# First layer of a two-layer encoder trunk: attention heads placed between quarters of the input and output projection

## What is computed

```python
h = rms_norm(x, ev_attn_norm)
proj = h @ ev_w_in                                # 1024 -> 2304 columns
a_q, a_k, a_v, b_q, b_k, b_v = jnp.split(proj, IN_SPLITS, axis=-1)
# mixer A: 8 query heads on 2 key heads, 64 wide, this and the previous chunk of 64, ALiBi, a sink per head
#   sc = (norm(q) . norm(k)) / 8 - slope * |i - j|;  p = exp(sc - m) / (sum + exp(sink - m));  o = p @ v
# mixer B: 8 heads, this chunk and all earlier ones, learned relative bias; softmax; o = p @ v
x = x + jnp.concatenate([out_a, out_b], axis=-1) @ ev_w_out
h = rms_norm(x, ev_ffn_norm)
x = x + swiglu(h, ev_w_gate, ev_w_up, ev_w_down)  # 1024 -> 2816 -> 1024
```

## Time and profile before

| | value |
|---|---|
| median of three runs | 1464.49 us (1462.91 to 1468.63) |
| the profiled execution, its time | 1464.81 us |
| its span, first to last instruction | 1462.9 us |
| TensorE busy share of the span | 95% |
| mean granted TensorE clock | 0.979 of full |
| last matmul of the input projection ends near | 67.6 us |
| first matmul of the output projection | 117.75 us |
| output projection ends near | 139.87 us |

### The profile page before, as it was taken

How to read it: one execution, slowest core, us unless ns; L and a number is a source line. 1 busy time by engine, 2 the same in 40 slices (tenths; PEclk the granted TensorE clock), 3 DMA queues, 4 the chain that set the end, 5 groups by cost and what they waited for, 6 DMA issues and landing times.

```text
span 1462.9 us, 19333 instructions
## 1 busy us (share of the span) xinstructions
PE 1387.6 (95%) x6469; PEld 1136.6 (78%) x6469; DVE 1168.6 (80%) x1452; ACT 1047.8 (72%) x1359; POOL 118.3 (8%) x181
## 2 busy tenths in 40 slices
PE   7999999998598599999999999999999999999997
PEld 5757788887466488888888888888888888888885
DVE  4775555545694699899989989989998998998996
ACT  4585544446494488787887887888788788788786
POOL 0100000000350530000000000000000000000000
PEclk9999999999799699999999999999999999999998
DMA  9806554212806499999999999999999999999980
GB/s 343 296 1 230 174 201 144 72 55 73 314 2 249 163 363 386 378 382 376 372 386 371 398 357 377 404 348 395 389 371 383 375 371 386 373 388 367 376 342 14
DMA packets 133186, 429.52 MB, mean 294 GB/s; under 512 B 4194, under 2 KB 11533, under 8 KB 133149
## 3 DMA queue, kind: packets, MB, share of 16 engines
q1 hardware_dynamic: 127696, 416.82, 75.2%
q0 software_dynamic: 2624, 9.47, 2.5%
q10 hardware_dynamic: 2828, 2.75, 0.6%
HBM read 422.73 MB, written 6.29 MB: 293 GB/s over the span
## 4 chain that ended last, share of the span: by engine, by line
PE 84%; issue 6%; DVE 5%; ACT 3%; DMA 1%; POOL 1%; ACTq 0%; SPq 0%; DVEq 0%; POOLq 0%
PE bank L604 26%; PE bank L606 26%; PE bank L605 26%; PE bank L566 2%; DVE w_lo L1264 1%; PE bank L669 1%; PE bank L697 1%; ACT w_hi L878 1%; PE bank L686 1%; PE bank L530 1%; DMA xres<-in_x_dram 1%; PE bank L680 1%; ACT hT_hi L906 0%; PE bank L679 0%; ACT h L916 0%
## 5 line engine op out<-in xcount | busy, mean ns | idle before, releaser
L1194 DVE TENSOR_TENSOR w_lo<-ring,w_hi 128x1024 fp32r<-128x1024 f32 x544 | 645.8, 1220 | 39.9 <-ACT w_hi L815 22.1
L815 ACT ACTIVATE w_hi<-ring 128x1024 fp32r<-128x1024 f32 x544 | 573.3, 1063 | 134.8 <-PE bank L606 134.5
L604 PE MATMUL bank<-w_hi,hT_hi 128*128 128x512 f32 (+3 forms) x1104 | 425.6, 385 | 8.3 <-DVE w_lo L1188 2.9
L605 PE MATMUL bank<-w_hi,hT_lo 128*128 128x512 f32 (+3 forms) x1104 | 423.9, 384 | 0.0
L606 PE MATMUL bank<-w_lo,hT_hi 128*128 128x512 f32 (+3 forms) x1104 | 423.8, 384 | 0.0
L604 PEld LDWEIGHTS bank<-w_hi,hT_hi 128*128 128x128 f32 x1104 | 208.5, 189 | 50.9 <-DVE w_lo L1264 4.5
L606 PEld LDWEIGHTS bank<-w_lo,hT_hi 128*128 128x128 f32 x1104 | 208.5, 189 | 40.7
L605 PEld LDWEIGHTS bank<-w_hi,hT_lo 128*128 128x128 f32 x1104 | 208.6, 189 | 40.1
L1264 DVE TENSOR_TENSOR w_lo<-ring,w_hi 128x1024 fp32r<-128x1024 f32 (+3 forms) x124 | 144.0, 1173 | 102.0 <-ACT w_hi L878 101.8
L878 ACT ACTIVATE w_hi<-ring 128x1024 fp32r<-128x1024 f32 (+3 forms) x124 | 121.1, 987 | 115.2 <-PE bank L606 110.1
L604 PE MATMUL bank<-w_hi,aT_hi 128*128 128x512 f32 x474 | 189.2, 399 | 10.0 <-issue 5.6
(11 more groups left out here) (246 smaller groups left out, 1175.1 us busy)
## 6 DMA issues: line engine op xcount, KB each, us to landing
ring<-in_od_e_gate_dram SPq DMA_DIRECT2D x57, 2048.0 KB, 9.4
ring<-in_od_e_up_dram SPq DMA_DIRECT2D x56, 2048.0 KB, 9.6
ring<-in_od_e_down_dram SPq DMA_DIRECT2D x56, 2048.0 KB, 9.8
ring<-in_ev_w_gate_dram SPq DMA_DIRECT2D x5, 2048.0 KB, 7.9
ring<-in_ev_w_up_dram SPq DMA_DIRECT2D x5, 2048.0 KB, 9.5
ring<-in_ev_w_down_dram SPq DMA_DIRECT2D x5, 2048.0 KB, 7.9
ring<-in_ev_w_in_dram SPq DMA_DIRECT2D x3, 2048.0 KB, 21.9
ring<-in_ev_w_out_dram SPq DMA_DIRECT2D x2, 2048.0 KB, 19.4
```

The lines of the kernel that those rows point to most:

```text
L604: pe.matmul(dst, hi, whi, start=first, stop=False)
L605: pe.matmul(dst, lo, whi, start=False, stop=False)
L815: act.activation(e_hi_at[place_of(q)], eights(ring[:, i % RING, j * QUARTER:(j + 1) * QUARTER]), ACT.Copy).then_inc(hi_ready, 1)
L1194: dve.tensor_tensor(e_lo_at[place_of(q)], eights(ring[:, i % RING, j * QUARTER:(j + 1) * QUARTER]), e_hi_at[place_of(q)].bitcast(F32), ALU ...
```

## The change

1. The input projection's columns are cut 512, 512, 512, 256, 512 (`IN_COLS`), so that everything but the B values is there after quarter 15. The first 16 quarters run as before, then `heads0()` replaces `attention(0, HEADS0)` on each engine. It puts the last four quarters of the input projection behind steps 0 to 3, and the eight quarters of the output projection behind steps 7, 9, 11, 13, 15, 17 and 20 (`SLOT`).
2. The output projection goes by rows: a quarter is 128 rows (two heads) by all 1024 columns, and its sums stay in banks 4 to 7 for all eight quarters. It waits only for its own two heads.
3. Queries and keys are transposed two heads at a time: a tile is 128 columns wide. With that, 26 transposes take the place of 64. The 16 heads share one bank for scores (bank 1), one for transposed q and k, one for transposed probabilities and one for outputs, since banks 4 to 7 are taken. A new semaphore, `score_taken`, holds the scores of a head until VectorE has read those of the head before.
4. The queries of mixer A are no longer multiplied by their norm; VectorE multiplies the scores by it together with adding the distance, in two instructions, and the slope goes into ScalarE's exponential.
5. The mask is added to the bias by VectorE between quarters 8 and 11 (`add_mask`), not by GpSimd.
6. The residual sums behind the output projection and behind the feed-forward part are made by halves: VectorE adds the left half when its last matmul is done (`first_half`). The order inside a quarter is changed to suit.
7. In `norm(1)` and `norm(2)` the first quarters of the next stage are split before the squares of the norm (`SPLIT_FIRST`).
8. The feed-forward pieces start at ring place 3, not 2, because place 2 is used as scratch for squares.

The core of the diff follows: the tables and the plan; `out_quarter` and `heads0` of TensorE; the end of a step of `heads0` on ScalarE and VectorE; `add_mask` and the residual sums on VectorE; the early split in `norm` on both.

```diff
+ORDER0 = (0, 1, 4, 5, 2, 3, 6, 7, 8, 9, 10, 11, 12, 13, 14, 15)
+TILE_STEP = {0: 0, 1: 1, 4: 2, 5: 3, 8: 4, 10: 5, 12: 6, 14: 7}
+IN_COLS = ((0, NW), (NW, NW), (2 * NW, NW), (3 * NW, NW // 2), (3 * NW + NW // 2, NW))
+SLOT = {0: (16,), 1: (17,), 2: (18,), 3: (19,),
+        7: (20,), 9: (21,), 11: (22,), 13: (23,), 15: (24,), 17: (25,), 20: (26, 27)}
...
-        add("out", cols(w["w_out"], j * NW, NW), KD, NW, j)
-    place = 2
+        add("out", w["w_out"][0, j * NW:(j + 1) * NW, :].rearrange("(k p) n -> p k n", p=P), 4, D, j, "rows", j)
+    place = 3
...
+            def out_quarter(q):
+                pe.wait_ge(o_lo, max(ORDER0.index(2 * k), ORDER0.index(2 * k + 1)) + 1)
+                hi, lo = (aT_hi, aT_lo) if k < 4 else (hT_hi, hT_lo)
+                product(q, lambda t, half: bank[4 + 2 * t + half], lambda _, t: hi[:, k, t * P:(t + 1) * P],
+                        lambda _, t: lo[:, k, t * P:(t + 1) * P])
...
+            def heads0():
+                for i in range(STEPS0):
+                    if i in TILE_STEP:
+                        for t in range(TB):
+                            mm = pe.transpose(bank[0][:, t * P:(t + 1) * P], q_pair(u, t), ident)
+                        if turns_k(u):
+                            for t in range(TB):
+                                mm = pe.transpose(bank[0][:, SEQ + t * P:SEQ + (t + 1) * P], k_pair(u, t), ident)
+                    n = i - 1
+                    if 0 <= n < HEADS0:
+                        pe.wait_ge(qkT_ready, 2 * u + 2)
+                        if n:
+                            pe.wait_ge(score_taken, n)
+                        pe.matmul(bank[1][:, 0:P], q[:, 0:P], k[:, 0:P], start=True, stop=True)
+                        pe.matmul(bank[1][:, P:LANES], q[:, P:SEQ], k, start=True, stop=True).then_inc(scored, 1)
+                    n = i - 4
+                    if 0 <= n < HEADS0:
+                        pe.wait_ge(p_ready, n + 1)
+                        if n:
+                            pe.wait_ge(pT_ready, n)
...
+                    for q in SLOT.get(i, ()):
+                        if q < pieces[4]["q1"]:
+                            in_quarter(q)
+                        else:
+                            out_quarter(q)
...
+                    for q in SLOT.get(i - 1, ()):
+                        if ends_piece(q):
+                            in_evict(quarters[q][0])
+                        split_to(q + LEAD)
...
+            def add_mask(raw, c0, keys):
+                m = cst[:, c0:c0 + keys][:, ::-1].unsqueeze(1).to_broadcast([P, B_HEADS, keys])
+                dve.tensor_tensor(raw, raw, m, ALU.add).then_inc(bias_ready, 1)
...
-                dve.wait_ge(quarter_used, p["q1"])
                 for half in range(2):
+                    if half == 0:
+                        dve.wait_ge(first_half, 2)
+                    else:
+                        dve.wait_ge(quarter_used, p["q1"])
                     for t in range(TB):
                         xs = xres[:, t, half * NW:(half + 1) * NW]
                         dve.tensor_tensor(xs, xs, bank[4 + 2 * t + half][:, :], ALU.add).then_inc(x_added, 1)
...
+        SPLIT_FIRST = {1: "ffn", 2: "dq"}
+                if n in SPLIT_FIRST:
+                    split_to(pieces[stage_pieces(SPLIT_FIRST[n])[0]]["q0"] + LEAD)
```

More of the change, by code:

```diff
@@ L97, in gain_rows @@
         g[row, 0:HD] = inputs[name][0]
+        g[row, HD:2 * HD] = inputs[name][0]
     for row, name in ((G_CQ, "od_q_norm"), (G_CK, "od_k_norm")):
@@ L132, in add @@
         first = len(quarters)
-        for k in range(0, nk, per):
+        for k in ROW_ORDER.get((stage, c), range(0, nk, per)):
             quarters.append((len(pieces), k, min(per, nk - k)))
@@ L356, in o_place, with o_place0, o_psum0, ends_piece @@
             return dst[r:r + 64, m // 2, :]
+        def o_place0(first, second, g):
+            r = 64 * (g % 2)
+            return (first if g < A_HEADS else second)[r:r + 64, g // 2, :]
+        def o_psum0(n):
+            r = 64 * (ORDER0[n] % 2)
+            return bank[3][r:r + 64, 0:SEQ]
+        def ends_piece(q):
+            return quarters[q][0] < 5 and q + 1 == pieces[quarters[q][0]]["q1"]
+        def slope(g):
+            return 2.0 ** (-8.0 * (g + 1) / A_HEADS)
+        def kT_of(u):
+            return kT0[:, 0 if u < A_KV * 2 else (u + 1) % 2, :]
+        def q_pair(u, t):
+            c = 2 * u * HD if u < A_HEADS // 2 else B_Q + (2 * u - A_HEADS) * HD
+            return proj[:, t, c:c + 2 * HD]
+        def in_copy(i, t):
+            n = lin[i]["n"]
+            dst, src = dest["in"](t, i, n), bank[4 + 2 * (i % 2) + t][:, 0:n]
+            if i == 0:
+                dst = dst.rearrange("p (g two d) -> p two g d", two=2, d=HD)
+                src = src.rearrange("p (two g d) -> p two g d", two=2, d=HD)
+            return dst, src
+        def k_pair(u, t):
+            c = A_K if u == 0 else B_K + (2 * u - A_HEADS) * HD
+            return proj[:, t, c:c + 2 * HD]
+        def v_of(n, t):
+            g = ORDER0[n]
+            c = A_V + g // (A_HEADS // A_KV) * HD if g < A_HEADS else B_V + (g - A_HEADS) * HD
+            return proj[:, t, c:c + HD]
+        def turns_k(u):
+            return u == 0 or u >= A_HEADS // 2
         def gate_bank(c):
@@ L421, in trunk @@
                   "uq": (2, lat_rinv, 1), "ukv": (4, lat_rinv, 1)}
+        HEAD_SUMS0 = 5
+        SPLIT_FIRST = {1: "ffn", 2: "dq"}
+        ROW_ENDS = [pieces[stage_pieces(s)[-1]]["q1"] - 1 for s in ("out", "ffn")]
         X_ADDS = {0: 0, 1: 4, 2: 8, 3: 12}
@@ L445, in _ @@
                     sp.wait_ge(pv_done, HEADS0)
+                if p["stage"] == "ffn" and p["place"] == 2:
+                    sp.wait_ge(head_ss, HEAD_SUMS0)
                 dst = ring[:, p["place"], 0:p["nk"] * p["n"]].rearrange("p (k n) -> p k n", k=p["nk"])
@@ L626, in flags @@
             def flags(p, k):
+                if p["kind"] == "rows":
+                    return k == 0 and p["c"] == 0, k == p["nk"] - 1 and p["c"] == 1
                 if p["kind"] != "down":
@@ L739, in _ @@
             turn_norm(0)
-            projection("in", sT(hT_hi), sT(hT_lo))
-            pe.wait_ge(queries_ready, 1)
-            attention(0, HEADS0)
-            pe.wait_ge(o_lo, HEADS0)
-            projection("out", sT(hT_hi), sT(hT_lo))
+            for q in range(IN_FIRST):
+                in_quarter(q)
+            heads0()
             turn_norm(1)
```

334 lines of the change are left out of this document (261 added, 73 removed).

## The result

The changed kernel takes 1459.45 us (median of 10 runs, 1456.13 to 1461.91) against 1463.70 for the kernel before beside it (10 runs). The ratio is 0.9957, 95% interval 0.9943 to 0.9972: faster by 0.3 to 0.6%, some 6 us by the ratio, while the two medians lie 4.3 us apart. The forecast was 1454.5. The profiled execution took 1459.23 us with a span of 1457.4, where the one of before had 1464.81 and 1462.9.

What follows compares the result with a forecast made beforehand. TensorE, busy 95% of the span, was taken as the bound. -8.7 us up to the output projection's end and -1.5 behind the feed-forward part made -10.2, giving 1454.5 us; own range 1452 to 1457, full range 1450.5 to 1461.

Steps and rivals of the forecast that it cites:

- rival (a): Heads, steps 4 to 7: TensorE's clock falls again, costing 3.4 us, total 1458; chance 0.15.
- if the clock is 0.50 in that stretch: Sign that the forecast is wrong: granted clock at 0.50 between 56 and 80 us, where nothing below 1.00 was expected.
- The ledger of the input projection, heads and output projection: Those three stages: 99.2 us dense plus 2.7 and 1.1 of stalls, 103.0 against 111.74, so -8.7 us.
- all of steps 4 to 7: First heads: TensorE waits 2.7 us before quarter 20, of which 1.7 for the single scores bank.
- in the tail: Last heads: probabilities of head 13 come 0.6 us late and head 15's wait 0.5, together 1.1 us.
- A pair of steps and a quarter: Steps 8 to 20: 7.6 us of TensorE against 6.0 of VectorE, so no stall.
- The clock: Input projection to output projection: granted clock assumed 1.00 throughout, so the old low stretch's 3.4 us count within -8.7.
- The halves and the early split: Behind the feed-forward part: 1.2 us from adding by halves, 0.3 from the early split, together -1.5 us.
- The mask: Input projection: 3.7 us on VectorE, quarter 15's split just in time, no stall; relieving VectorE of GpSimd's contention gains 0.
- (c): Heads: single banks cost a handover of 0.3 us per step, 6.3 us over 21 steps, total 1461; chance 0.13.
- (d): Head loop: eleven uncovered splits cost 25 us, total 1480; chance 0.06.
- (e): Heads: output projection quarters fill nothing, only transposes (4.6 us) and 1.5 are gained, near 1458.5; chance 0.04.

Runs made afterwards that it cites:

- Experiment 11: The changed kernel run once more, unaltered: 1458.73 us (11 runs); its profiled run had the same wait but no fall of the clock.
- experiment 1: Changed kernel plus five 512-column matmuls that nothing reads, ahead of the wait in head step 6: 1456.23 us, ratio 0.9935 to the kernel before.
- experiment 2: Changed kernel plus 3, 3 and 5 matmuls that nothing reads in head steps 4, 5 and 6: 1457.31 us, ratio 0.9941 to the kernel before.
- experiment 12: Changed kernel plus two matmuls that nothing reads ahead of the wait in head step 6: 1455.93 us, ratio 0.9929 to the kernel before.
- experiment 5: Changed kernel with no quarters between the heads, plus 4, 4, 4, 4 and 2 unread matmuls in steps 1 to 5: 1460.27 us (12 runs).
- experiment 6: Changed kernel with quarters 16 to 19 and 25 to 27 spread over other head steps, plus four unread matmuls in step 2: 1457.71 us.
- experiment 7: Changed kernel with the feed-forward end as before (residual added whole, no early split there): 1458.98 us (12 runs).
- experiment 9: Changed kernel with bias and mask added on GpSimd again instead of VectorE: 1461.97 us (12 runs).
- experiment 8: Changed kernel with the feed-forward end as before, plus five unread matmuls in head step 6: 1457.70 us (6 runs).
- experiment 3: Changed kernel with quarters 16 to 19 behind head steps 0, 1, 3 and 5 instead of 0 to 3: 1456.00 us, ratio 0.9932 to the kernel before.
- experiment 4: Changed kernel with no quarters between the heads, twenty in front and eight behind: 1474.47 us, ratio 1.0045 to the kernel before.

## Why the prediction was right, and where it was off

**The number.** 1459.45 us lies inside the stated range of 1450.5 to 1461, but not inside the 1452 to 1457 given for the forecast itself, and the gain, 4.3 us by the medians and some 6 by the ratio, is about half of the 10.2 us forecast. It is inside because the range covered rival (a), which is also what the profile shows. The stretch from 77.6 us on at 0.51 is one of the prediction's own signs of being wrong ("if the clock is 0.50 in that stretch", 56 to 80).

**The ledger of the input projection, heads and output projection** held. It gave 103.0 us, 99.2 dense and 3.8 of stalls. Experiment 11's last row above, from the same start to the first mark, has 103.82, of which 100.10 busy and 3.72 idle. Each stall is where it was put: 1.46 and 0.30 in step 6 and ahead of it (1.7 was said for the one, 2.7 for all of steps 4 to 7; idle in 55.80 to 77.56 are 2.0), 0.82 and 0.79, 1.6 together, in the tail (1.1 said). That the sums agree to 0.1 us is in part luck: one stall was smaller than said and the other larger. A pair of steps and a quarter take 7.65 us (7.6 said), and no wait stands between quarters 20 and 25. What is over is 0.9 us of busy time, which I did not trace further.

**The clock** is the step that failed: "The clock's 3.4 us are in that, since I assume 1.00 throughout". In the profiled run rival (a) happened, 6.8 us at 0.51 for 3.0 us (first marks 134.82 and 131.82 of the two runs of one kernel). It was given 0.15 against 0.50 for the forecast, with rows that speak both ways; it should have had as much. Fillings in front of the wait (experiments 1, 2 and 12) keep the clock at 1.00 in all three traces and bring the first mark to 131.45 to 133.00. Nor was its counterpart certain in the kernel before: the one trace had the fall, but by the mean clock 29 of 79 runs seem not to. Like with like, by the mean clock of the run: at 0.981 and 0.982, 1456.2 (6 of the 21 runs of the changed kernel) against 1462.6 (11), -6.4; at 0.979, 1459.4 (6 runs) against 1464.4 (5), -5.0. (The runs of the kernel before are those beside experiments 5, 6, 7 and 9, on another chip; on the chip of experiment 11 alone, 1456.6 in 4 runs stands against 1462.8 in 3.) Of the forecast's -10.2 the 3.4 are then hardly a part of the change, and -6.8 stand against -6.4 and -5.0. The predicted 1454.5 is the sum against a trace with the fall; the runs that keep the clock are at 1456.2. Of the other 1.7 us, 0.9 is the busy time above, and the rest is of the size of the time given back, below.

**The halves and the early split**, -1.5: the marks say -0.98 and -0.46, experiment 8 says 1.5 us. The first is 0.2 short of the 1.2: VectorE's additions begin at 325.27, behind a split of 0.96 us (from 324.39) that the forecast did not have there; that this is the reason was not tried. Mechanism and size were right.

**The mask**: on VectorE it takes 3.5 us (3.7 said), the split for quarter 15 is in time, and there is no wait. "Relieving VectorE gives nothing there" was true of the order before and false of the new one: experiment 9 lost 2.5 us, 1.9 of it by the first mark. What became of the rest was not traced. The move was needed for the rest of the gain. The prediction had only priced it against the old trace, where four quarters of lead covered the slow split.

**Not foreseen**: of the time gained by the third mark part is given back behind it. From there to the mark that waits 5.25 us in TensorE's queue pass 28.97 us before, 29.57 in the changed kernel and 30.13 in experiment 11:

```profile
375.08 0.77 PE L681 MATMUL bank<-w_hi,aT_hi 128*128 128x512 f32 x1 [5.25 <-issue]
```

Two explanations offer themselves: an earlier start meets a wait that does not move, or the clock is lower there. The windows of this stretch decide it. Kernel before, experiment 11, experiment 12:

```profile
351.80:380.77 28.97, 20.70 (x89) 16.70 (x89) 19.52 (x39) 16.69 (x33) 5.69 (x6) 0.92 0.56 191
342.56:372.69 30.13, 21.86 (x88) 17.55 (x89) 19.51 (x39) 16.68 (x33) 5.68 (x6) 0.83 0.54 184
342.19:371.04 28.85, 20.58 (x89) 16.62 (x89) 19.52 (x39) 16.68 (x33) 5.69 (x6) 0.92 0.56 192
```

Experiment 12 starts earliest of all and gives nothing back. TensorE's idle time is 8.27 us in each of the three; only its busy time differs, and it goes with the granted clock. So it is in all 14 traces: idle 8.25 to 8.27 us; at 0.92 or 0.93 the stretch takes 28.85 to 29.09 us, at 0.83 to 0.89 29.57 to 30.30. The time given back is the clock again, 0.6 to 1.3 us of it, in a stretch whose code did not change. Why the clock is lower there in some runs stays open.

**The other rivals**: (c), single banks with 0.3 us a step, did not happen while quarters stand between the heads; with the quarters away and the clock kept it is at most the 3.9 us of experiment 5, which hold the start and the tail of the heads too. (d) and (e) did not happen: steps 8 to 16 have no wait.

## What to carry to other kernels

A stretch in which TensorE is 100% busy can be at half its clock: read the granted clock of each stage beside its busy share, and when a wait of a microsecond stands ahead of a long run of short matmuls, try spare real work (or as a test, matmuls that nothing reads) in it. In the kernel before, the same filling won nothing in the median. When a forecast books or spends clock time, look at the spread of run times of both kernels for two groups before trusting one trace, and keep that term apart from the change. A transfer of work off an engine is to be priced in the new order, with the lead that is left there, not in the old trace.

## What the hardware showed that I had not expected

- The same program with the same wait (1.45 and 1.46 us) kept its clock in one run and lost it in the other for 6.8 us, 3.0 us of time.
- The length of one wait does not decide: 2.02 us at 69.25 in experiment 5 was followed by 1.00, the 1.46 us at 76.55 by 0.51. A wait of 0.93 us in step 2 was followed by 0.52 over 65.8 to 69.3 in experiment 3 and by 1.00 in experiment 6.
- The level lasts. The same head work ran at 0.50 for some 40 us in experiment 4 and at 1.00 in experiment 5, which had entered it at full clock. The Trainium skill ("TensorE: Matmul & The Clock Gate", Part 4 on transposes) says that a transpose does not engage the full clock and does not count as PE-busy in the same way. With 8 or 10 transposes among the 24 or 26 matmuls that the timeline shows for two heads, experiment 4 would agree, and experiment 5, at 1.00 with the same ones, shows that this alone does not settle the level. What ended the low stretch in experiment 4 near 119 us, and after 6.8 us in the kernel before, stays open.
